# Channel mixers of a decoder trunk: chunk loops written out on two engines, table work placed inside chunks, weight sums moved ahead, head and end of each mixer reordered

## The reference

```python
def swiglu(x, w_in, w_out):
    gate, up = jnp.split(x @ w_in, 2, axis=-1)
    return (jax.nn.silu(gate) * up) @ w_out
...
    for l in range(DEPTH):
        x = layer_norm(ALPHA * x + 0.5 * swiglu(x, ffn1_w_in[l], ffn1_w_out[l]), ...)
        if l % 2 == 0:
            y = diff_pool_mixer(x, cos, sin, ...)          # differential attention and pooling
        else:
            y = hgrn2_mixer(x, c_w_in[j], c_w_o[j], c_norm[j], lower_bounds[l])
        x = layer_norm(ALPHA * x + y, ...)
        x = layer_norm(ALPHA * x + 0.5 * swiglu(x, ffn2_w_in[l], ffn2_w_out[l]), ...)
```

## Time and profile before

| | us |
|---|---|
| median of 3 runs | 1027.21 (1026.97 to 1028.56) |
| the profiled execution | 1028.77 |
| its span, first to last instruction | 1027.0 |
| PE busy | 971.7 |
| DVE busy | 849.5 |
| ACT busy | 587.8 |

### The profile page before, as it was taken

One profiled execution on the slowest core, in us unless ns is written; L12 is line 12 of the kernel. 1 busy time (PEld: TensorE's weight loads), 2 busy tenths in 40 slices (PEclk: granted clock), 3 DMA queues, 4 the chain that ended last, 5 costly groups with the idle time before them and its releaser, 6 DMA issues.

```text
span 1027.0 us, 13044 instructions
## 1 busy us (share of the span) xinstructions
PE 971.7 (95%) x4520; PEld 798.6 (78%) x4520; DVE 849.5 (83%) x1204; ACT 587.8 (57%) x643; POOL 35.9 (3%) x63
## 2 busy tenths in 40 slices
PE   9489999999998999998979999989999998999997
PEld 7368888778886788887758888878788886888885
DVE  5568878896788888889897887899998887788887
ACT  6366656534735666654355555646888725555550
POOL 0100000000210000000000000000000100000000
PEclk9889999999999999999989999999999999999999
DMA  8536765645356566666345666645422664655641
GB/s 288 170 100 202 271 204 173 223 144 199 104 200 247 174 196 203 197 212 205 123 162 171 207 196 205 207 162 164 149 99 94 211 202 149 201 179 196 207 158 41
DMA packets 129260, 184.77 MB, mean 180 GB/s; under 512 B 5953, under 2 KB 104785, under 8 KB 129089
## 3 DMA queue, kind: packets, MB, share of 16 engines
q1 hardware_dynamic: 126032, 173.56, 51.0%
q0 software_dynamic: 2624, 10.11, 2.7%
q10 hardware_dynamic: 560, 0.52, 0.2%
...
HBM read 183.13 MB, written 1.05 MB: 179 GB/s over the span
## 4 chain that ended last, share of the span: by engine, by line
PE 77%; DVE 13%; ACT 5%; DMA 3%; issue 2%; POOL 0%; SPq 0%; DVEq 0%; ACTq 0%; POOLq 0%
PE psum L1662 24%; PE psum L1664 23%; PE psum L1663 23%; DVE w_lo L921 3%; PE psum L1795 1%; ACT w_hi L480 1%; DMA raw<-in_ffn_w_in 1%; PE psum L2134 1%; DVE w_lo L949 1%; DVE x_tok L1026 1%; DMA cols<-in_diff_subln 1%; DVE x_tok L1036 1%; PE psum L2120 1%; DVE arena L1319 1%; DVE hT_lo L968 0%
## 5 line engine op out<-in xcount | busy, mean ns | idle before, releaser
L1662 PE MATMUL psum<-w_hi,xT 128*128 128x512 f32 x959 | 380.6, 397 | 20.5 <-ACT arena L525 18.4
L1664 PE MATMUL psum<-w_hi,xT 128*128 128x512 f32 x959 | 375.5, 392 | 0.0
L1663 PE MATMUL psum<-w_lo,xT 128*128 128x512 f32 x959 | 375.2, 391 | 0.0
L921 DVE TENSOR_TENSOR w_lo<-raw,w_hi 128x2048 fp32r<-128x2048 f32 x125 | 284.8, 2283 | 8.3 <-ACT w_hi L480 8.1
L480 ACT CAST w_hi<-raw 128x2048 fp32r<-128x2048 f32 x125 | 238.4, 1914 | 25.9 <-DMA raw<-in_ffn_w_in 8.9
L1662 PEld LDWEIGHTS psum<-w_hi,xT 128*128 128x128 f32 x959 | 181.2, 189 | 63.8 <-issue 22.8
L1664 PEld LDWEIGHTS psum<-w_hi,xT 128*128 128x128 f32 x959 | 181.0, 189 | 38.5
L1663 PEld LDWEIGHTS psum<-w_lo,xT 128*128 128x128 f32 x959 | 181.3, 189 | 36.3
L517 ACT ACTIVATE ffn_tok<-psum 128x256 f32<-128x256 f32 x88 | 33.7, 383 | 226.7 <-PE psum L1664 226.7
L1662 PE MATMUL psum<-w_hi,hT_hi 128*128 128x512 f32 x316 | 130.6, 413 | 24.5 <-DVE w_lo L949 11.9
L1664 PE MATMUL psum<-w_hi,hT_lo 128*128 128x512 f32 x316 | 125.1, 396 | 0.0
...
## 6 DMA issues: line engine op xcount, KB each, us to landing
...
```

The lines of the kernel that those rows point to most:

```text
L921: nc.vector.tensor_tensor(w_lo[:, slot_of[n]], raw[:, n % RAW], w_hi[:, slot_of[n]].bitcast(F32), ALU.subtract).then_inc(lo_ready, 1)
L1662: nc.tensor.matmul(dst, a_hi, b_hi, start=first, stop=False)
L1663: nc.tensor.matmul(dst, a_hi, b_lo, start=False, stop=False)
L1664: return nc.tensor.matmul(dst, a_lo, b_hi, start=False, stop=last)
```

## The change

- DVE and ACT: the loop over chunks 2 to 9 is written out; the plain blocks of chunk c's unit are now split at the end of chunk c. ACT does this ahead of silu 1, DVE behind the unit rest. Weight sums wait for the landing of the unit alone. PE and SP keep their loops, and SP waits for sums and plain rest.
- PE: product 2 moves ahead of the projection of tile 1; in the head product 4 moves behind the transposes.
- Head: weight sums, and the split of the sums, are made earlier; blocks of chunk 0 come ahead of the two unit rests; the copy of chunk 1 comes ahead of the plain split.
- Tables: `beside` puts rotary angles into chunks 4 to 6 of F0, the decay copy into chunk 3 and the softmax arguments into chunks 4 to 7 of F1, the lower bound into chunks 3 to 6 of F2, each ahead of multiply 0. Sin and Exp move to the start of AB, the softmax Exp to the head of F2. Masks are loaded as bytes and no longer cast. POOL's loads wait for one unit less.
- End: one product bank is copied and added within chunk 9, the other adds are spread; the norm's gain comes ahead of multiply 1, its scale ahead of the last rest of tile 1.

```diff
--- before.py
+++ after.py
...
+                    sp.wait_ge(plain_lo, last if i is None else i * 2 + last)
                 else:
                     sp.wait_ge(lo_ready, last if i is None else i * 4 + last)
...
@@ -542,61 +543,61 @@
                     split_hi(s0 + 3)
                     split_plain_hi(s0 + 4)
                     hidT_copy(name, 0, T[0])
+                    split_sums_hi(name, s0 + 4)
                     hid_blocks_hi(name, 0)
                     act.wait_ge(hid_ready, hid + 1)
                     ffn_silu(name, 0, 1, G[0])
-                    split_sums_hi(name, s0 + 4)
+                    split_hi(s0 + 5)
                     act.wait_ge(hid_ready, hid + 2)
                     ffn_silu(name, 1, 1, G[1])
-                    split_hi(s0 + 5)
                 else:
                     xT_split(m, 0)
                     split_hi(s0 + 3)
+                    if name == BEFORE_C:
+
+                        act.wait_ge(S["bound_args"], 4)
+                        nc.scalar.activation(gam, gam, ACT.Exp).then_inc(S["bound_exps"], 1)
                     ffn_silu(name, 0, 0, G[0])
+                    split_plain_hi(s0 + 4)
                     xT_split(m, 1)
                     act.wait_ge(hid_ready, hid + 1)
                     ffn_silu(name, 0, 1, G[1])
-                    split_plain_hi(s0 + 4)
+                    split_sums_hi(name, s0 + 4)
+                    split_hi(s0 + 5)
                     ffn_silu(name, 1, 0, G[0])
-                    split_hi(s0 + 5)
                     hidT_copy(name, 0, G[0])
                     hid_blocks_hi(name, 0)
-                    split_sums_hi(name, s0 + 4)
                     act.wait_ge(hid_ready, hid + 3)
                     ffn_silu(name, 1, 1, G[1])
                 split_hi(s0 + 6)
-                if name == BEFORE_AB:
-
-                    act.wait_ge(S["angles_ready"], 1)
-                    nc.scalar.activation(sincos, ang[:, 4:6].rearrange("p a (t f) -> p a t f", t=TT), ACT.Sin
-                                         ).then_inc(S["sincos_ready"], 1)
-                    act.wait_ge(S["lambda_products"], 1)
-                    nc.scalar.activation(lam[:, 2:4], lam[:, 0:2], ACT.Exp).then_inc(S["lambda_exps"], 1)
-                if name == "F1" and BEFORE_C:
-
-                    act.wait_ge(S["bound_args"], 2)
-                    nc.scalar.activation(gam, gam, ACT.Exp).then_inc(S["bound_exps"], 1)
-                with act.Fori(0, NPAIR) as i:
-                    for par in range(2):
-                        n, c = s0 + 7 + 3 * par, i * 2 + (2 + par)
-                        split_plain_hi(n, i)
+                hidT_copy(name, 1, G[0])
+                split_plain_hi(s0 + 7)
+                last = NC - 2
+                for c in range(2, NC - 1):
+                    n = s0 + 3 * c + 1
+                    if c > 2:
                         hidT_copy(name, c - 1, G[0])
-                        split_hi(n + 1, i)
-                        hid_blocks_hi(name, c - 1)
-                        ffn_silu(name, 0, c, G[0])
-                        split_sums_hi(name, n, i)
-                        split_hi(n + 2, i)
-                        ffn_silu(name, 1, c, G[0])
+                    split_hi(n + 1)
+                    hid_blocks_hi(name, c - 1)
+                    ffn_silu(name, 0, c, G[0])
+                    split_sums_hi(name, n)
+                    split_hi(n + 2)
+                    if c == last:
+                        act.wait_ge(plain_used, N_PROD * (f + 1))
+                        nc.scalar.activation(kept[0], PROD[0], ACT.Copy, scale=NORMS[name][1]).then_inc(copied_out, 1)
+                        split_hi(n + 3)
+                    else:
+                        split_plain_hi(n + 3)
+                    ffn_silu(name, 1, c, G[0])
 
                 n, c = s0 + FFN_UNITS - 1, NC - 1
-                split_hi(n - 1)
+                act.wait_ge(pairs_done, f + 1)
+                nc.scalar.activation(SUM_PLACES[name][:, 0], PROD[4], ACT.Copy, scale=NORMS[name][1]
+                                     ).then_inc(copied_out, 1)
                 hidT_copy(name, c - 1, G[0])
                 act.wait_ge(hidT_copied, N_COPY * (f + 1))
                 act.wait_ge(sums_used, N_PROD * (f + 1))
                 nc.scalar.copy(hT_hi[:, 0], hid_blocks[:, 0:512]).then_inc(hidT_hi, 1)
-                factor = NORMS[name][1]
-                nc.scalar.activation(kept[0], PROD[0], ACT.Copy, scale=factor).then_inc(copied_out, 1)
-                nc.scalar.activation(kept_last, PROD[4], ACT.Copy, scale=factor).then_inc(copied_out, 1)
                 split_hi(n)
                 split_hi(n + 1)
...
+                act.wait_ge(S["angles_ready"], 1)
+                nc.scalar.activation(sincos, ang[:, 4:6].rearrange("p a (t f) -> p a t f", t=TT), ACT.Sin
+                                     ).then_inc(S["sincos_ready"], 1)
+                act.wait_ge(S["lambda_products"], 1)
+                nc.scalar.activation(lam[:, 2:4], lam[:, 0:2], ACT.Exp).then_inc(S["lambda_exps"], 1)
...
                 if part == 0:
-                    dve.wait_ge(plain_hi, nth_now)
+                    dve.wait_ge(raw_landed[n % RAW], 32 * (n // RAW))
...
@@ -1053,139 +1058,144 @@
                     ffn_hidden(name, 0, G[0], 0, ffn_tok[:, 1, 0])
                     ffn_hidden(name, 1, G[1], 1, ffn_tok[:, 1, 1])
                     split_lo(s0 + 3)
+                    weight_sums(name, s0 + 4, 0)
+                    weight_sums(name, s0 + 4, 1)
+                    hidden_sums(name, 0)
                     split_plain_lo(s0 + 4)
-                    hidden_sums(name, 0)
-                    weight_sums(name, s0 + 4, 0)
                     hid_blocks_lo(name, 0)
-                    weight_sums(name, s0 + 4, 1)
                     ffn_hidden(name, 0, G[0], 2, ffn_tok[:, 0, 0])
                     split_sums_lo(name, s0 + 4)
                     ffn_hidden(name, 1, G[1], 3, ffn_tok[:, 0, 1])
-                    split_lo(s0 + 5)
                 else:
                     xT_split(m, 0)
                     norm(ORDER[m - 1], 1)
                     ffn_hidden(name, 0, G[0], 0, ffn_tok[:, 1, 0])
                     split_lo(s0 + 3)
                     xT_split(m, 1)
+                    weight_sums(name, s0 + 4, 0)
+                    weight_sums(name, s0 + 4, 1)
                     ffn_hidden(name, 0, G[1], 1, ffn_tok[:, 0, 0])
                     split_plain_lo(s0 + 4)
-                    if name == "F1" and BEFORE_C:
-                        lower_bound_max()
-                    if name == BEFORE_C:
-                        lower_bound(1)
+                    split_sums_lo(name, s0 + 4)
                     ffn_hidden(name, 1, G[0], 2, ffn_tok[:, 1, 1])
-                    if name == "F1" and BEFORE_C:
-                        layer_c_tables()
-                    weight_sums(name, s0 + 4, 0)
                     hidden_sums(name, 0)
-                    weight_sums(name, s0 + 4, 1)
                     hid_blocks_lo(name, 0)
-                    split_lo(s0 + 5)
                     ffn_hidden(name, 1, G[1], 3, ffn_tok[:, 0, 1])
-                    split_sums_lo(name, s0 + 4)
-                    if name == "F1" and BEFORE_C:
-                        lower_bound_arg(0)
-                        lower_bound_arg(1)
+                split_lo(s0 + 5)
                 split_lo(s0 + 6)
-                if name == BEFORE_AB:
-                    rope_tables()
-                if name == "F1" and BEFORE_C:
-                    lower_bound(0)
-                if name == BEFORE_C:
-                    lower_bound(2)
-                    lower_bound(3)
-                with dve.Fori(0, NPAIR) as i:
-                    for par in range(2):
-                        n, c = s0 + 7 + 3 * par, i * 2 + (2 + par)
-                        split_plain_lo(n, i)
+                hidden_sums(name, 1)
+                split_plain_lo(s0 + 7)
+                last = NC - 2
+                for c in range(2, NC - 1):
+                    n = s0 + 3 * c + 1
+                    if c > 2:
                         hidden_sums(name, c - 1)
-                        weight_sums(name, n, 0, i)
-                        hid_blocks_lo(name, c - 1)
-                        weight_sums(name, n, 1, i)
-                        ffn_hidden(name, 0, G[0], c * 2, ffn_tok[:, 1, 0])
-                        split_lo(n + 1, i)
-                        split_sums_lo(name, n, i)
-                        ffn_hidden(name, 1, G[0], c * 2 + 1, ffn_tok[:, 1, 1])
-                        split_lo(n + 2, i)
+                    weight_sums(name, n, 0)
+                    hid_blocks_lo(name, c - 1)
+                    weight_sums(name, n, 1)
+                    beside(name, c)
+                    ffn_hidden(name, 0, G[0], c * 2, ffn_tok[:, 1, 0])
+                    split_lo(n + 1)
+                    split_sums_lo(name, n)
+                    if c == last:
```

(72 more changed lines are left out.)

143 lines of the change are left out of this document (68 added, 75 removed).

## The result

The changed kernel takes 1009.94 us (median of 4 runs, 1009.05 to 1014.09); the kernel before took 1027.88 in the same runs. The ratio is 0.9833, with an interval of 0.9804 to 0.9863: faster by 18 us, where 32 were forecast. (One later execution of the same kernel took 1618.12 us at a mean granted clock of 0.556; no median in this document holds it.) The profiled execution took 1010.16 us.

What follows compares the result with a forecast made beforehand. PE's idle time at heads and ends was to be had; chunks could not become shorter. Heads -38.3, loops -1.4, beside work +10.5, ends -3.05 gave -32.3 us: 994.9 us as a median, range 985 to 1005.

Steps and rivals of the forecast that it cites:

- the wait on the copy: F0's head: PE's 16.46 us standstill until 55.60 goes, as the table work leaves the place.
- F1's five parts: Table work in F1's chunks: the decay copy costs 0.3 us, four softmax parts 0.25 each; +1.3 us.
- the ends with AB and C: Ends of the four mixers: -3.05 us in sum; AB's constants, Sin and Exp lie in waits: 0.
- Rival A: Table work beside the chunks is free since DVE idles in every chunk: 984.4 us; chance 0.10.
- The weakest step named: Chunk 2: unit 8's load waits for unit 5's rest and ACT holds the blocks behind it.
- No such gap reaches 2.7, so I take no slow clock.: Chunks with table work: PE's gaps, 2.15 us for a lower-bound part, bring no clock of 0.50.
- rival D: Four heads: a longer gap in chunk 2 brings the slow clock back, 3 us each: 1007 us; chance 0.04.
- the second gap: Chunk 2: PE waits for the blocks' rest, 2.2 us in F0, 1.9 in F3.
- the slack of silu 1 behind the plain cast: Chunks: the cast delays silu 1 by at most 0.2 us, multiply 1 at 14.1, wanted at 14.3; taken as 0.
- rival C: Plain load ahead of silu 1 lands late, costing 0.3 us in each of 32 chunks: 1004.5 us; chance 0.08.
- POOL's earlier loads beside unit 6: 0: POOL's earlier loads run beside unit 6, which has 3 us to spare, so they cost 0.
- Rival E: F2's head: table switch with a pause as long as the load delays silu 0 by 2.2 us: 997.1; chance 0.04.

Runs made afterwards that it cites:

- the second one: The changed kernel as it is, run again for a second profiled execution: 1010.92 us, ratio 0.9813.
- The made gaps: Kernel with all three follow-up edits, plus one useless DVE instruction ahead of multiply 0 in chunks 3 to 9, its length set per mixer: 1055.29 us.
- the second experiment: The changed kernel with ACT's plain cast for the next chunk behind silu 1 instead of ahead of it (chunks 2 to 8): 1009.2 us, ratio 0.9803.

## Why the prediction was right and wrong

**Right.** The bound and the places: chunk 2 of F0 starts at 37.19 (forecast 37.3) and the wait on the copy is gone; no table load is left in the chunks, and where neither table work nor a late load stands, F0's and F1's chunks take 16.1 us; multiply 0 of a chunk with a lower-bound part is late by 1.95 to 2.18 us (forecast 2.15); F1's five parts cost 0.35 each (forecast 0.3 and four times 0.25); the ends with AB and C gave 3.0 (forecast 3.4); product 2 ahead of tile 1 costs nothing of its own (16.13 us a plain chunk in either place, with silu 1 ahead of the cast). Rival A was wrong: work in front of multiply 0 isn't free. Its condition, the idle time ahead of multiply 1, is real, and using it gave the largest part of the further gain. The weakest step named, ACT holding the blocks behind unit 8, happened in all four mixers.

**Wrong: "No such gap reaches 2.7, so I take no slow clock."** This step missed 5.1 us in the profiled execution (chunks 3 to 5 of F2 against chunk 6). In the second one six stretches follow instead of three, and three of them stand in heads, which is rival D's mechanism, in three mixers. I had read a bound off a few gaps of one trace, and not all of them: of its two gaps of 3.06 us, the one that ends at 862.57 is followed by a fall and the one that ends at 520.65 is not. The made gaps show no sharp bound, with none behind 1.6 us and less, and some behind 1.8.

**Mis-sized: the second gap.** Taken as 2.2, 1.9, 1.9 and the same for F3, measured 2.07, 2.14, 3.51 and 2.07. The excess is F2's load, 6.8 us from its first issue to its last landing where I took 5.4. And every gap costs some 0.3 us more than its idle time: chunk 6 of F2, at full clock, takes 18.38 us with a gap of 1.95, and chunk 2 of F1 18.56 with one of 2.14, where a plain chunk takes 16.12. (The idle time is counted from the end of a matmul's record, 0.39 us long, while matmuls start every 0.227; and the first one behind a gap takes 0.50, as at 587.90.) Four heads make 1.2 us of this.

**Wrong: the slack of silu 1 behind the plain cast.** I gave it 0.2 us in steady chunks, and there it holds. In chunk 2 the plain unit is issued later against PE, since it waits for the weight sums: 0.60 us in F0, 0.75 in F2. That is rival C's mechanism at a place where I hadn't looked. In F1 there is no such wait (its transposes follow at once), and in F3 it is 0.1; the 0.3 and 0.5 that I named for them ahead of the second experiment are mostly the 0.3 of each gap. The second gap (1.9 in all over the forecast), the 0.3 of each gap and this (1.4) are 4.5 of the 5.3 us that the heads lack; the rest I can't place.

**Left out: POOL's second group.** "POOL's earlier loads beside unit 6: 0" named the seven small loads only. The wait of the four large ones also counts one rest less, and they moved from the middle of chunk 4 to its start, ahead of the plain unit's load. The chunk takes 2.06 us more than a plain one; 1.6 of it went with silu 1 ahead of the cast, the rest is the angles'. That the loads are what made the unit land late is argued from their times alone; silu ahead of the cast showed that a late landing costs nothing by itself.

**Rival E.** In F2's head the softmax Exp takes two switches of tables (ACT):

```profile
470.03 1.28 ACT L559 ACT_TABLE_LOAD   x1
471.33 1.92 ACT L559 ACTIVATE arena<-arena 128x2048 f32<-128x2048 f32 x1
473.26 1.28 ACT L518 ACT_TABLE_LOAD   x1
474.56 0.39 ACT L518 ACTIVATE ffn_tok<-psum 128x256 f32<-128x256 f32 x1
```

Each next instruction starts within 0.02 us of the load's end. The drain of about 1.38 us per switch that the Trainium skill states (ScalarE: Activation LUTs, What ACT_TABLE_LOAD costs) is not seen in either switch, so E falls.
